# Two-layer decoder trunk, one core: q and k of the stick-breaking mixer transposed by DMA instead of TensorE, its scores and sums two steps later

## What is computed

```python
for l in range(DEPTH):                      # 2 layers
    xn = _rms_norm(x, attn_norm_g[l])
    (sb_q, sb_k, sb_v, df_q, df_k, df_v, mb_q, mb_k, mb_v, ns_q, ...) = split(xn @ w_in[l])
    o_a = _stick_breaking(heads(sb_q), heads(sb_k), heads(sb_v))      # mixer A
    o_b = _diff_attention(rope(norm(df_q)), rope(norm(df_k)), df_v)   # mixer B
    o_c = _moba(...)                                                  # mixer C
    o_d = _nsa(...)                                                   # mixer D
    merged = sum(sigmoid(xn @ w_gate[l, i] + b_gate[l, i]) * (o @ w_branch[l, i]) ...)
    x = x + merged @ w_out[l]
    hn = _rms_norm(x, ffn_norm_g[l])
    x = x + (silu(hn @ w_ffn_gate[l]) * (hn @ w_ffn_up[l])) @ w_ffn_down[l]

def _stick_breaking(q, k, v):               # per head: 256 x 64
    z = (q @ k.T) / sqrt(64)
    log1m = where(kpos < qpos, log_sigmoid(-z), 0)
    between = reverse_cumsum(log1m) - log1m
    a = where(kpos < qpos, exp(log_sigmoid(z) + between), 0)
    return a @ v
```

## Time and profile before

| what | value |
| --- | --- |
| runs | 827.54, 827.85, 828.66 us; median 827.85 |
| profiled execution | 828.2 us; span of its instructions 826.4 us |
| TensorE busy | 821.6 us, 99% of the span |
| VectorE busy | 559.7 us, 68% |
| ScalarE busy | 477.8 us, 58% |
| GpSimd busy | 293.7 us, 36% |
| DMA | 167.76 MB, mean 203 GB/s |
| granted clock of TensorE | 1.00 |

### The profile page before, as it was taken

One profiled execution on the slowest core, in us unless ns is written; L12 is line 12 of the kernel. 1 busy time (PEld: TensorE's weight loads), 2 busy tenths in 40 slices (PEclk: granted clock), 3 DMA queues, 4 the chain that ended last, 5 costly groups with the idle time before them and its releaser, 6 DMA issues.

```text
span 826.4 us, 11044 instructions
## 1 busy us (share of the span) xinstructions
PE 821.6 (99%) x4050; PEld 673.7 (82%) x4050; DVE 559.7 (68%) x821; ACT 477.8 (58%) x715; POOL 293.7 (36%) x297
## 2 busy tenths in 40 slices
PE   9999999999999999999999999999999999999998
PEld 5888888888888888888888888888788888888886
DVE  5576889868865666655454688898697666666542
ACT  6886655785465554543457775567844645454441
POOL 0078784404303432320000889653061044323100
PEclk9999999999999999999999999999999999999999
DMA  9745877684558777785565556878745687877652
GB/s 332 271 138 178 222 230 219 182 247 131 203 178 229 199 230 212 223 221 183 167 203 195 162 192 192 224 222 210 223 153 178 206 214 218 230 223 212 215 184 71
DMA packets 119637, 167.76 MB, mean 203 GB/s; under 512 B 56608, under 2 KB 59040, under 8 KB 119328
## 3 DMA queue, kind: packets, MB, share of 16 engines
q1 hardware_dynamic: 119296, 166.79, 66.9%
q10 hardware_dynamic: 288, 0.27, 0.1%
HBM read 153.40 MB, written 1.05 MB: 187 GB/s over the span
## 4 chain that ended last, share of the span: by engine, by line
PE 98%; DMA 1%; issue 0%; SPq 0%; ACT 0%; DVE 0%
PE acc L732 91%; PE att L812 1%; PE att L895 1%; PE att L779 1%; PE att L886 1%; DMA w_raw<-in_w_in 1%; PE att L804 1%; PE acc L812 1%; PE att L853 0%; PE att L869 0%; PE att L908 0%; PE att L972 0%; PE att L963 0%; PE att L854 0%; PE att L839 0%
## 5 line engine op out<-in xcount | busy, mean ns | idle before, releaser
L1234 DVE TENSOR_TENSOR w_lo<-w_raw,w_hi 128x1024 fp32r<-128x1024 f32 (+1 forms) x276 | 365.4, 1337 | 147.1 <-ACT w_hi L996 144.6
L732 PE MATMUL acc<-w_hi,xt 128*128 128x512 f32 (+1 forms) x1728 | 432.3, 392 | 0.5 <-ACT xt L1019 0.3
L996 ACT ACTIVATE w_hi<-w_raw 128x1024 fp32r<-128x1024 f32 (+1 forms) x275 | 286.1, 1051 | 168.7 <-PE acc L732 159.1
L732 PEld LDWEIGHTS acc<-w_hi,xt 128*128 128x128 f32 x1728 | 319.0, 188 | 66.3 <-issue 1.3
L732 PE MATMUL acc<-w_lo,xt 128*128 128x512 f32 (+1 forms) x864 | 229.9, 388 | 0.0
L732 PEld LDWEIGHTS acc<-w_lo,xt 128*128 128x128 f32 x864 | 162.0, 188 | 32.9
L1485 POOL TENSOR_SCALAR small<-small 128x2 f32<-128x2 f32 (+4 forms) x14 | 10.4, 745 | 209.2 <-ACT sq_dump L1096 132.4
L1617 POOL COPY hid_t<-hid_halves_t 128x512 uint16<-128x512 uint16 x44 | 37.7, 885 | 94.3 <-DMA hid_halves_t<-hid_halves 80.0
L1608 POOL COPY hid_halves<-hid 128x512 uint16<-128x512 uint16 x44 | 45.6, 1064 | 65.2 <-DVE hid L1311 65.2
L1625 POOL TENSOR_TENSOR merged<-merged,prod 128x1024 f32<-128x1024 f32 x10 | 32.5, 3250 | 61.2 <-DVE prod L1283 60.3
L732 PE MATMUL acc<-w_hi,ht_hi 128*128 128x512 f32 x176 | 47.7, 390 | 0.0
(11 more groups left out here) (175 smaller groups left out, 723.5 us busy)
## 6 DMA issues: line engine op xcount, KB each, us to landing
w_raw<-in_w_ffn SPq DMA_DIRECT2D x88, 512.0 KB, 4.2
w_raw<-in_w_gate SPq DMA_DIRECT2D x64, 512.0 KB, 3.9
w_raw<-in_w_ffn_down SPq DMA_DIRECT2D x44, 512.0 KB, 4.0
w_raw<-in_w_in SPq DMA_DIRECT2D x39, 512.0 KB, 4.7
w_raw<-in_w_branch SPq DMA_DIRECT2D x16, 512.0 KB, 4.1
w_raw<-in_w_out SPq DMA_DIRECT2D x16, 512.0 KB, 3.3
bg<-in_b_gate SPq DMA_DIRECT2D x8, 512.0 KB, 5.4
w_raw<-in_w_in SPq DMA_DIRECT2D x8, 396.0 KB, 3.4
```

What stands on the lines that cost most here:

```text
L732: return pe.matmul(acc[bank0 + t][:, 0:N], x_part[:, k0 + k, t * P:(t + 1) * P], w_part[:, k, 0:N], start=first, stop=last)
L996: act.activation(w_hi[:, n % WR, :, 0:N], w_raw[:, n % RAW, :, 0:N], copy).then_inc(s_hi, 1)
L1234: dve.tensor_tensor(w_lo[:, n % WR, :, 0:N], w_raw[:, n % RAW, :, 0:N], w_hi[:, n % WR, :, 0:N].bitcast(F32), ALU.subtract).then_inc(s_lo, 1)
```

## The change

Steps Aq and Ak are gone. Mixer A uses `deal` (u = 4) and `join` (u = 9), with SP's DMA transposes ahead of its load of chunk 12. GpSimd multiplies q of mixer A by 1/8 in place before the deal, which ScalarE's copy did in passing. Steps z and sp move from u = 9 and 14 to 11 and 16, cum from 13 and 17 to 15 and 19. The load of `cw` moves from u = 12 to u = 20.

```diff
-TURN_AT = {33: "C", 40: "D"} | {CHUNKS.index(("ffn", j, 3)) + 9: j for j in range(N_FFN)}
+TURN_AT = {12: "A", 33: "C", 40: "D"} | {CHUNKS.index(("ffn", j, 3)) + 9: j for j in range(N_FFN)}
...
-    ... "Aq": 6,
-    "Ak": 7, "Az": (9, 14), "Asp": (9, 14), "Acum": (13, 17), "Apv": (21, 21), "Bq": 19, "Bk": 20,
+    ... "Adeal": 4,
+    "Ajoin": 9, "Az": (11, 16), "Asp": (11, 16), "Acum": (15, 19), "Apv": (21, 21), "Bq": 19, "Bk": 20,
...
-    for name in ("Aq", "Ak", "Bq", "Bk", "Dc"):
+    for name in ("Bq", "Bk", "Dc"):
         put(PLAN[name], "qk", name)
-    for mixer in "CD":
+    for mixer in "ACD":
         for kind in ("deal", "join"):
             put(PLAN[mixer + kind], kind, mixer)
...
-                    if u == 12:
+                    if u == 20:
...
                         sp.dma_start(cw[:, :, :, :], cmp_w[l]).then_inc(s_cw, 16)
...
                 if n == 0:
-                    if mixer in "CD":
+                    if mixer != "B":
                         pe.wait_ge(joined.sem, joined.at(l, ("join", mixer)))
...
                         elif kind == "deal":
-                            if a == "C":
-                                srcs = [(proj[:, :, MBQ:MBQ + 2 * MIX], 0, 2 * MIX)]
+                            if a == "A":
+                                pool.wait_ge(proj_out.sem, proj_out.at(l, ("proj", 0)))
+                                settled(pool.tensor_scalar(proj[:, :, SBQ:SBQ + MIX], proj[:, :, SBQ:SBQ + MIX],
+                                                           HD ** -0.5, None, ALU.mult))
+                            if a != "D":
+                                c0 = SBQ if a == "A" else MBQ
+                                srcs = [(proj[:, :, c0:c0 + 2 * MIX], 0, 2 * MIX)]
```

More of the change, by code:

```diff
@@ L86 @@
     "stats": 1, "stats_f": 3, "lambda": 14, "x": (0, 0, 1, 2), "f": (-2, -1, 2, 3), "m": (-1, -1, 2, 3),
-    "sig": (49, 53, 57, 57), "o": (22, 45, 48, 58), "subln": 40, "prep": (13, 18, 25), "ngate": 25, "Aq": 6,
-    "Ak": 7, "Az": (9, 14), "Asp": (9, 14), "Acum": (13, 17), "Apv": (21, 21), "Bq": 19, "Bk": 20,
+    "sig": (49, 53, 57, 57), "o": (22, 45, 48, 58), "subln": 40, "prep": (13, 18, 25), "ngate": 25, "Adeal": 4,
+    "Ajoin": 9, "Az": (11, 16), "Asp": (11, 16), "Acum": (15, 19), "Apv": (21, 21), "Bq": 19, "Bk": 20,
     "Bsm": (21, 21, 27, 27), "Bp": (21, 24, 27, 29), "Bpt": (24, 27, 29, 32), "Bpv": (27, 29, 33, 35), "Bo": 36,
@@ L530, in turned @@
         def turned(l, what):
-            if what in ("C", "D"):
-                return 16 * NT * (2 * l + "CD".index(what) + 1)
+            if what in ("A", "C", "D"):
+                return 16 * NT * (3 * l + "ACD".index(what) + 1)
             return 16 * NT * (l * len(range(what % 2, N_FFN, 2)) + what // 2 + 1)
@@ L627, in _ @@
                     if u in TURN_AT:
-                        (turn if TURN_AT[u] in ("C", "D") else turn_hid)(l, TURN_AT[u])
+                        (turn if TURN_AT[u] in ("A", "C", "D") else turn_hid)(l, TURN_AT[u])
                     if chunk(l, u) > 2:
@@ L785, in qk @@
                 bank_free(l, step)
[L786 to L790, removed]
+                if name == "Dc":
                     pe.wait_ge(act_misc.sem, act_misc.at(l, ("ngate", None)))
@@ L793, in qk @@
                     pe.wait_ge(pool_done.sem, pool_done.at(l, ("prep", name[0])))
-                c0 = {"Aq": SBQ, "Ak": SBQ + MIX, "Bq": DFQ, "Bk": DFK, "Cq": MBQ, "Ck": MBK,
-                      "Dq": NSQ}.get(name)
+                c0 = {"Bq": DFQ, "Bk": DFK}.get(name)
                 for m in range(2):
                     for t in range(NT):
-                        if name == "Dk":
-                            src = kdup[:, t, 2 * m:2 * m + 2, :]
-                        elif name == "Dc":
+                        if name == "Dc":
                             src = kcdup[:, t, m, :, :]
@@ L1034, in qk_copy @@
                 m = 0 if name[1] == "q" else 2
-                act.activation(qkt[name[0] in "BD"][:, m:m + 2, :].rearrange("p m t -> p (m t)"), att[:, TP, :], copy,
-                               scale=HD ** -0.5 if name == "Aq" else 1.0).then_inc(read_act.now(step), 1)
+                act.activation(qkt[1][:, m:m + 2, :].rearrange("p m t -> p (m t)"), att[:, TP, :], copy
+                               ).then_inc(read_act.now(step), 1)
             def pt_free(l, step):
@@ L1569, in _ @@
                             pool.wait_ge(s_turn, turned(l, a))
-                            last = {"C": ("z", PAIRS["A"] - 1), "D": ("sm", ("B", PAIRS["B"] - 1))}[a]
-                            pool.wait_ge(att_done.sem, att_done.at(l, last))
+                            last = {"A": ("sm", ("C", PAIRS["C"] - 1)), "C": ("z", PAIRS["A"] - 1),
+                                    "D": ("sm", ("B", PAIRS["B"] - 1))}[a]
+                            if l or a != "A":
+                                pool.wait_ge(att_done.sem, att_done.at(l - (a == "A"), last))
                             for t in range(NT):
```

## The result

The changed kernel takes 831.02 us (median of 7 runs, 829.79 to 831.65) where the kernel before takes 828.0 us (827.54 to 828.66): 1.0034 times as long, 95% interval 1.0023 to 1.0046. It is slower by 3.0 us. The forecast was +1.5 us, in a range that holds the result.

A forecast was written before the change was run, and what follows sets the result against it. TensorE, busy 99% of the span, bounds the kernel. Transposes -1.9, waits at Bq +1.1 and +2.3 give +1.5 us: 829.7 from the profiled 828.2, 829.4 against the median 827.85, stated as 829.5; range 826.6 to 832.9.

The forecast's parts named there:

- The transposes, 0.95 us a layer: TensorE, chunks 5 to 8: removing two groups of four transposes saves 0.95 us a layer, 1.90 for both.
- Prep B starts later by 1.2 and 2.2 us, at 47.7 and 457.6: GpSimd's prep B, layers 0 and 1: starts 1.2 and 2.2 us later because the first z's chain moves.
- Prep B lasts 16.6 us: GpSimd's prep B: 14.5 us undisturbed plus 2.1 us lost to VectorE's work, instead of 18.44 and 18.51 before.
- the rate of 0.75 us for each us of VectorE's work: GpSimd during prep B: loses 0.75 us per us of VectorE's work; 2.7 us of work cost 2.1 us.
- The 17.2 us that the rule of a full lock would give: Prep B's length if GpSimd lost all 2.7 us of VectorE's work; the sum would be 1.2 us higher.
- TensorE waits 1.1 and 2.3 us at Bq: TensorE at step Bq: waits for GpSimd's prep B, 1.1 us in layer 0 and 2.3 us in layer 1.
- Costed at nothing: Scaling, deal, DMA transposes, chunk 12's load and cw's new place: no time added; chunk 12 lands by 39, wanted at 41.9.
- its bound of 1.04: GpSimd's scaling of q before the deal: between nothing and about 1.04 us, a two-operand multiplication of that size.
- rival (c): First z in layer 0 waits for the join, up to 2 us late: 829.4 to 831.4; chance 15%, at 830.5.
- the clock, rival (d): TensorE's waits lower its clock: one chunk at half speed per layer adds 2 x 2.73 us, 834.9; chance 5%.

The follow-up runs named there:

- e3: Kernel before with only z, sp and cum of mixer A moved two chunks later, TensorE's transposes and cw's load kept in place: 832.68 us (1.0056).
- e6: Changed kernel with the second z and sp at u = 18 and the second cum at 20, so sp falls behind prep B: 829.46 us (1.0017).
- e10: As e9, with VectorE's sum of squares for prep B ahead of its split of chunk 14 instead of behind it: 827.98 us (1.0).
- e1: Changed kernel with the second cum ahead of step Bq instead of behind it, on TensorE and ScalarE: 827.16 us (0.9992).
- e4: Changed kernel with 16 products that nobody reads ahead of Bq's wait in layer 1 alone: 829.46 us (1.0019).
- e7: Changed kernel with cw loaded at u = 12 again, as in the kernel before: 831.97 us (1.0043).
- e2: Changed kernel with Bq, Bk and the first scores and first p of mixer B one chunk later: 835.94 us (1.0102).
- e5: Changed kernel with z, sp and cum one chunk later than in the kernel before, instead of two: 827.35 us (0.9992).
- e9: As e5, with q of mixer A scaled by 1/8 on ScalarE instead of GpSimd: 827.66 us (0.9997).

## Why the prediction was right, and where it was short

- *The transposes, 0.95 us a layer.* 0.96 and 0.97; with them put back (e3) the stretch is as before. Right, and not hidden.
- *Prep B starts later by 1.2 and 2.2 us, at 47.7 and 457.6.* It started at 47.20 and 457.25, in an execution whose chunk 3 is 0.5 us early. The chain of waits has the links that were named: z's chain, sp, one split, the sum.
- *Prep B lasts 16.6 us.* 16.58 and 16.48. For the work that was reckoned with, which meets the last operations of prep B, the rate of 0.75 us for each us of VectorE's work is borne out by taking some of it away (e6): 0.70 to 0.75. It is no rate for VectorE's work in general. The reckoning passed over the splits that meet prep B's first operations, in both kernels, and gave no reason; three of them inside L1479 made no difference, one across the start of the same operation cost 0.84 us (e10), and that no split lay there in either kernel is luck. The 17.2 us that the rule of a full lock would give ("SBUF — State Buffer" of the Trainium skill, section "SBUF: two separate sides") were not reached. GpSimd's start behind VectorE's split in e10 is like that rule; that VectorE's splits inside GpSimd's L1479 took their usual 1.2 us is not, so the measurement stands between no lock and a lock for each whole instruction.
- *TensorE waits 1.1 and 2.3 us at Bq.* 1.00 and 2.17 by the list. e1, e3 and e4 show that this is the whole place of the loss.
- *Costed at nothing.* The scaling took 1.50 us, above its bound of 1.04, and the deal 3.43 instead of 3.90, so that SP issued at 27.86, near the 28.2 reckoned. The load of chunk 12 did not stop TensorE, and the join in layer 0 ended at 35.20, 1.9 us ahead of z: rival (c) did not happen. ScalarE did wait up to 3.13 us for chunks, which I had not looked at. It cost nothing here, and e7 shows how near that was: I had taken the move of `cw` as free, and not as the thing that keeps the first z's chain on time.
- *The step that was mis-sized: the clock, rival (d).* The sum had no term for it, and the rival had 5% and a price of 5.5 us over both layers. In fact a wait of 2.17 us, which the forecast itself contained, brought the clock down in layer 1 and cost 1.51 us; the wait of 1.00 us in layer 0 cost none. That is the whole difference between the forecast of +1.5 and the +3.0 measured; the one run of the seven with a mean clock of 1.000 took 829.79 us, 0.3 above the forecast of 829.5. The cost belonged into the forecast with a share of its own as soon as a wait of over 2 us stood in it. The Trainium skill's page "TensorE: Matmul & The Clock Gate", Part 1, was cited for exactly this, that the array falls to half its clock when it has been idle for long enough. The traces agree that an idle stretch can bring the clock down to the lower level, 0.50 behind the 2.17 us and 1.00 behind the 1.00 us; but the fall came 1.5 us after the products had begun again, and a pause of the same 2.17 us in e7 brought none.

## What to carry to other kernels

When the bounding engine has under half a microsecond of slack at a hand-over, making it faster is worth nothing until the producer is earlier too, and a step that is moved must be followed through every in-order queue it now stands ahead of: here ScalarE's chain for z and VectorE's sp moved ahead of the sum that GpSimd's work hung on. Look for work of the waiting engine that is ready and can stand ahead of the wait; one such swap (e1) recovered 3.9 us, where shifting the consumer (e2) only opened the next wait. A wait of some 2 us on TensorE should be priced at more than its length, for the clock behind it.

## What the runs showed of the hardware

Pauses of 1.00 us (changed kernel), 1.07 us (e1) and 1.12 us (e6) left TensorE's granted clock at 1.00. Pauses of 2.15 to 2.17 us did so in e3 and in layer 1 of e7, and brought it down to the lower level for a while in the changed kernel and in layer 0 of e7, where the means of the next 5 us are 0.65 and 0.67. After 3.02 us in e2 the next products ran at full speed, after 3.54 us they did not. Small products that nobody reads kept the clock at 1.00 (e4). How much VectorE slows GpSimd depends on the operation that it meets: three splits inside a GpSimd operation of 5.46 us made no difference, one across the start of the same operation cost 0.84 us, and two rotations of 0.29 us became 1.01 and 1.27 us. GpSimd's scaling of 128 x 512 by a constant took 1.50 us, above the bound of 1.04 us that the prediction gave it. Two DMA transposes cost SP 2.72 us to issue when they stood 2.9 us behind a chunk's load (e5), and 4.03 us when they stood 0.9 us behind one (e9).
